# Dilated attention's query, key and value projections as seven block products, with the token sums on GpSimd

## The chip, the cores and the metric

One core of a Trainium2 chip runs the whole program. The metric is device microseconds of one execution; the kernel before was timed three times: 3373.47, 3375.91 and 3383.08 us, median 3375.91 us. All data are float32. In the trace a float32 matmul shows as two weight loads and two matmul passes (records of PEld and PE), so a count of passes is twice a count of matmuls.

## The reference, cut to what matters

The program computes two transformer blocks. The change lies in the second, where one 512 x 1024 activation `h` is multiplied by a wide weight matrix, and nine slices of 512 columns of the product are the dilated attention's queries (three slices), keys (three) and values (three); queries and keys are then turned by rotary angles.

```python
def rope(x, pos):
    hd = x.shape[-1]
    inv = ROPE_THETA ** (-jnp.arange(0, hd, 2, dtype=jnp.float32) / hd)
    ang = pos.astype(jnp.float32)[..., None] * inv
    ...
    return jnp.concatenate([x1 * cos - x2 * sin, x2 * cos + x1 * sin], axis=-1).astype(x.dtype)

def dilated_branch(dq, dk, dv, pos):
    B, S, _ = dq.shape
    shp = (B, S, DIL_GROUPS, DIL_HEADS, DIL_HD)
    q = rope(dq.reshape(shp), pos)
    k = rope(dk.reshape(shp), pos)
    v = dv.reshape(shp)
    ...

def second_block(x, positions, w_in, ...):
    for l in range(DEPTH_2):
        h = rmsnorm(x, pre_mix_g[l])
        z = h @ w_in[l]
        (g_q, g_k, g_v, g_o, a_low, sc_b, sc_c, sc_x,
         d_q, d_k, d_v) = jnp.split(z, split_points, axis=-1)
        y_gla = gla_branch(g_q, g_k, g_v, g_o, a_low, w_alpha_up[l], b_alpha[l], gla_norm_g[l])
        y_sc = sc_b * causal_dwconv(sc_c * sc_x, sc_conv_w[l])
        y_dil = dilated_branch(d_q, d_k, d_v, positions)
        ...
```

## The kernel before, in words

The program is a row of phases. Each phase is one block with a hand-written instruction list for each engine, and the engines meet between two phases. The last four phases are, with their stretches in the trace: `recurrent_phase` (L2007, to about 2326 us), `rope_phase` (L2406, 2326.8 to 2574), `merge_phase` (L2471, to 2882) and `feed_forward_phase` (L2692, from 2884 to the end).

`hT` holds the activation transposed: 128 partitions x 8 contraction blocks x 512 tokens. `ring` has two slots, each a weight job of 128 x 8 x 512 (2 MB). Jobs 0 to 5 are used in the recurrence, jobs 6 to 14 (`ROPE_JOB` = 6) in `rope_phase`, jobs from 15 (`GATE_JOB`) in the merge. SyncE issues job j once the last product of job j-2 is finished (L2424 to L2426).

`rope_phase` has 36 units, four to a job. The 24 query and key units have 128 weight columns as the stationary operand and 512 tokens as the moving one; the 12 value units have 128 tokens stationary and 512 weight columns moving. Each unit is eight matmuls over the contraction blocks into one of two PSUM banks `pa` (L2439, L2441). Of a query or key unit ScalarE copies the two halves of 64 partitions crosswise into `xs` (L2451, L2452), VectorE multiplies PSUM by `cos` (L2464) and `xs` by `sin` (L2465) and adds the two into `QK` (L2468). Of a value unit ScalarE copies PSUM to `dv` (L2456).

In `recurrent_phase` GpSimd clears two buffers and then, for each of four token tiles t, copies four diagonal blocks of `red` to `ST` (L2075) when VectorE has reduced them (L2283). TensorE runs the 128x512 products of jobs 2 to 5 (L2086) between the small products of the recurrence (L2121 to L2128, L2139 to L2146); its `weigh(t)` waits for the copies of tile t, for the state update (L2292, L2294) and for the norm (L2301, L2303) of tile t-1.

`merged` is a buffer of 128 x 8 x 512 that is first written in the merge phase.

The feed-forward phase of the kernel before already multiplies in the manner of the change: each of its 22 units is 28 matmuls of 128x256, seven products P1 to P7 of four contraction blocks each (L2824), from sums of weight blocks (VectorE L2983; for the first pair of units GpSimd L2751) and sums of token blocks. ScalarE copies P1 (L2906), and four VectorE additions of 512, 256, 512 and 512 elements (L2971 to L2974) make four output blocks of the seven products.

## Time and profile before

| what | value |
|---|---|
| three runs, median | 3375.91 us (3373.47 to 3383.08) |
| the profiled execution | 3380.27 us, its span 3378.5 us |
| TensorE matmul busy | 2861.0 us, 85% of the span |
| TensorE weight loads busy | 1655.1 us, 49% |
| VectorE busy | 1158.2 us, 34% |
| ScalarE busy | 767.0 us, 23% |
| GpSimd busy | 529.3 us, 16% |
| mean granted TensorE clock | 0.947 |

All numbers of the trace are of the one profiled execution. PE is TensorE's matmul record, PEld its weight load, DVE VectorE, ACT ScalarE, POOL GpSimd, SP SyncE; L2439 is line 2439 of the kernel. A time at which a row of the timeline starts is counted from the start of the span. Records that follow one another on an engine are merged into one row; the row's length is then that of the whole run of records, with the modelled end of the last. What stands in brackets is the idle time of the engine before the row and what released it.

### The profile page before, as it was taken

What the parts mean: (1) busy time and instruction counts of PE and PEld (TensorE: products, weight loads), DVE (VectorE), ACT (ScalarE), POOL (GpSimd) and SP (SyncE); (2) the same over time, 40 slices, a digit from 0 to 9 for tenths busy, and PEclk for the clock granted to TensorE, in tenths of its full rate; (3) what the DMA queues carried; (4) which work ended last, traced back from release to release, by engine and by line L of the source; (5) the groups of instructions that cost most, each with busy time, mean ns of one, the idle gap of its engine ahead of it and who ended that gap; (6) DMA issues with size and microseconds to landing.
All of it is one profiled execution on the core that took longest, in us unless ns stands there. A gap on an engine that the chain in (4) does not pass through costs nothing. (4 is left out here: it accounts for less than half of the span.)

```text
span 3378.5 us, 52188 instructions
## 1 busy us (share of the span) xinstructions
PE 2861.0 (85%) x21441; PEld 1655.1 (49%) x21441; DVE 1158.2 (34%) x2400; ACT 767.0 (23%) x1507; POOL 529.3 (16%) x660
## 2 busy tenths in 40 slices
PE   7998889588776798895867573999999999999999
PEld 4555655344343345653433332444444554588844
DVE  3424866312111343754111113533211231355501
ACT  2224651121111323630211112311112231111100
POOL 0003630233332001521322221000000000100000
PEclk8999999799999899996989886999999999999999
DMA  8733012999999552026999997112222112422337
GB/s 299 310 148 117 1 76 94 385 396 425 426 426 410 218 125 98 1 100 258 384 424 422 425 424 277 64 51 83 75 75 75 50 50 75 113 75 75 124 125 261
DMA packets 188531, 679.18 MB, mean 201 GB/s; under 512 B 52766, under 2 KB 94222, under 8 KB 163782
## 3 DMA queue, kind: packets, MB, share of 16 engines
q1 hardware_dynamic: 176446, 655.56, 49.9%
q0 software_dynamic: 11808, 21.03, 1.7%
q8 instruction: 131, 2.15, 0.3%
q14 instruction: 42, 0.34, 0.0%
q10 hardware_dynamic: 104, 0.10, 0.0%
HBM read 653.89 MB, written 33.98 MB: 204 GB/s over the span
## 5 line engine op out<-in xcount | busy, mean ns | idle before, releaser
L1719 PE MATMUL pH<-w,room 128*32 128x256 f32 x4224 | 253.3, 394 | 56.1 <-DMA w<-in_moe_w 55.6
L1756 DVE TENSOR_TENSOR hh<-hs,pH 128x128 f32<-128x128 f32 x118 | 34.0, 288 | 775.1 <-ACT hs L1739 775.1
L1719 PE MATMUL pH<-room 128*32 128x256 f32 x3328 | 211.7, 412 | 89.9 <-DMA room<-in_moe_w 66.9
L942 POOL TENSOR_SCALAR E<-E,st 128x768 f32<-128x768 f32 (+3 forms) x80 | 168.2, 2102 | 646.7 <-DVE st L1192 646.0
L1719 PEld LDWEIGHTS pH<-w,room 128*32 128x32 f32 x4224 | 140.9, 114 | 159.6 <-issue 79.3
L419 PE MATMUL pa<-aT,w 128*128 128x512 f32 x416 | 205.8, 599 | 1.3 <-DVE aT L693 1.3
L1719 PEld LDWEIGHTS pH<-room 128*32 128x32 f32 x3328 | 114.5, 119 | 179.7 <-issue 95.6
L1727 PE MATMUL pY<-w,hT 128*32 128x256 f32 x2112 | 130.4, 388 | 77.6 <-DVE hT L1759 60.9
L2534 PE MATMUL pa<-hT,ring 128*128 128x512 f32 x384 | 167.8, 592 | 0.0
L2439 PE MATMUL pa<-hT,ring 128*128 128x512 f32 x384 | 165.0, 592 | 1.3 <-PEq L91 1.3
L987 PE MATMUL pT<-ident,E 128*128 128x128 f32 x672 | 112.6, 286 | 55.0 <-ACT PT L1097 31.3
L2868 PE MATMUL banks<-ring,aT 128*128 128x512 f32 x352 | 151.2, 592 | 0.0
L1727 PE MATMUL pY<-room,hT 128*32 128x256 f32 x1664 | 100.6, 382 | 54.3 <-DVE hT L1759 54.3
L2086 PE MATMUL pa<-hT,ring 128*128 128x512 f32 x320 | 143.9, 606 | 0.0
L1017 PE MATMUL pS<-wout,oT 128*128 128x512 f32 x320 | 141.4, 594 | 0.8 <-issue 0.8
L1675 POOL DMA_INDIRECT y<-y,at_y x122 | 125.8, 1031 | 60.2 <-POOL at_y L1695 59.1
L1739 ACT ACTIVATE hs<-pH 128x128 f32<-128x128 f32 x118 | 32.7, 277 | 450.9 <-PE pH L1719 450.9
L1727 PEld LDWEIGHTS pY<-w,hT 128*32 128x32 f32 x2112 | 63.2, 111 | 144.0 <-DVE hT L1759 105.7
L1742 ACT ACTIVATE y<-pY 128x256 f32<-128x256 f32 x118 | 45.2, 383 | 346.5 <-PE pY L1727 343.7
L987 PEld LDWEIGHTS pT<-ident,E 128*128 128x128 f32 x672 | 71.2, 142 | 100.2 <-issue 47.6
L2439 PEld LDWEIGHTS pa<-hT,ring 128*128 128x128 f32 x384 | 72.9, 190 | 93.4 <-issue 93.4
L956 PE MATMUL pS<-room 64*128 64x256 f32 (+2 forms) x608 | 109.6, 477 | 8.3 <-ACT E L1086 4.9
(532 smaller groups left out, 4497.6 us busy)
## 6 DMA issues: line engine op xcount, KB each, us to landing
w<-in_moe_w SPq DMA_DIRECT2D x144, 2048.0 KB
room<-in_moe_w SPq DMA_DIRECT2D x48, 2048.0 KB
mw<-in_mod_w SPq DMA_DIRECT2D x24, 2048.0 KB, 16.6
ring<-in_w_ff_down SPq DMA_DIRECT2D x33, 1024.0 KB, 4.8
ring<-in_w_in SPq DMA_DIRECT2D x15, 2048.0 KB, 8.2
ring<-in_w_gate SPq DMA_DIRECT2D x6, 2048.0 KB, 8.4
wf<-in_w_ff_gate SPq DMA_DIRECT2D x11, 1024.0 KB, 5.7
wf<-in_w_ff_up SPq DMA_DIRECT2D x11, 1024.0 KB, 8.1
```

Of the source, the lines that this page charges most:

```text
L419: last = pe.matmul(pa[n % 2][:, 0:512], w[:, i % SLOTS_W, k, tile(c)], aT[:, k, 0:512], start=(k == 0), stop=(k == C - 1))
L942: pool.tensor_scalar(e, e, st[:, u % 4, 6 + b:7 + b], None, ALU.mult).then_inc(readyP, 1)
L956: return pe.matmul(pS[u % 2][:, at:at + w], qT[rows, p, tile(n)], kT[rows, k_chunk(p), k0:k0 + w], start=True, stop=True)
L987: last = pe.transpose(pT[:, tile(j)], E[:, u % NB, b, tile(i)], ident[:])
L1017: last = pe.matmul(pS[n % 2][:, half * 512:(half + 1) * 512], oT[:, k, tile(n)], wout[:, k, half * 512:(half + 1) * 512], start=(k == 4), ...
L1675: pool.indirect_dma_start(out=y_rows, out_offset=bass.IndirectOffsetOnAxis(ap=at_y[:, b:b + 1], axis=0), in_=y[:, b], in_offset=None, boun ...
L1719: last = pe.matmul(pH[strip(s), 0:2 * P].rearrange("p (j n) -> p j n", j=2), xT[:, k, :], slot_of(g, "w13", b)[:, :, k, s * P:(s + 1) * P] ...
L1727: last = pe.matmul(pY[strip(s), 0:YW], hT[:, k, :], slot_of(g, "w2", b)[:, k, s * YW:(s + 1) * YW], start=(k == 0), stop=(k == HC - 1))
L2086: last = pe.matmul(pa[b][:], ring[:, j % RING, i, tile(c)], hT[:, i, :], start=(i == 0), stop=(i == C - 1))
L2439: last = pe.matmul(pa[b][:], ring[:, j % RING, i, at], hT[:, i, :], start=(i == 0), stop=(i == C - 1))
L2534: last = pe.matmul(pa[b][:], ring[:, j % RING, k, (c % 4) * P:(c % 4 + 1) * P], hT[:, k, :], start=(k == 0), stop=(k == C - 1))
L2868: last = pe.matmul(banks[b][:, h * 512:(h + 1) * 512], aT[:, f, tile(t)], wd[:, m % SLOTS_D, f % 2, h * 512:(h + 1) * 512], start=(f == 0) ...
```

## The change

`rope_phase` is rewritten. A job's eight contraction blocks are split into `lo` and `hi`, its 512 weight columns into two halves, the 512 tokens into two halves. A job is now two units b = 0, 1 (128 columns of each column half; for the values 128 tokens of each token half). Each unit is seven products of four matmuls of 128x256, 28 matmuls in all, and gives the four 128x256 output blocks that two units gave before. The factors are blocks of `ring` and of `hT`, three sums of weight blocks in `S`, a fourth sum written over a weight block in place, and four sums of token blocks in `T`, which lies in `merged`.

VectorE makes the weight sums of a job (four additions of 128x1024; for the first job eight of 128x512) and turns each unit's seven products into outputs with four additions (`post`) in `Z`. Queries and keys are turned by three VectorE operations of 128x1024 for each unit, from `Z` instead of from PSUM, with two ScalarE copies of 64x1024 crosswise in between. Values go from `Z` to `dv` by two ScalarE copies. The four token sums are made by GpSimd in the recurrence, behind its copies of tile 1. `xs` and `Z` are single buffers, PSUM is double (two tensors of 1024 for each b). A ring slot is reloaded when `raised[1]`, the last product of its job, is counted.

```diff
--- before.py
+++ after.py
@@ -2004,7 +2004,7 @@
     return 16 * (j // RING + 1)
-def recurrent_phase(nc, g, hT, yT, cos, sin, rc):
+def recurrent_phase(nc, g, hT, yT, cos, sin, rc, T):
     BLK = 32
     SHORT = 6 * 2 * BLK
@@ -2035,8 +2035,8 @@
             ph.sem(n) for n in ("a_low", "a_moved", "raised", "logs", "rel", "exped", "inputs"))
         k_turned, k_moved, scored, d_taken, upper, reduced, diag_moved = (
             ph.sem(n) for n in ("k_turned", "k_moved", "scored", "d_taken", "upper", "reduced", "diag_moved"))
-        weighed, kv, stated, squared, meaned, rooted, normed, order_a = (
-            ph.sem(n) for n in ("weighed", "kv", "stated", "squared", "meaned", "rooted", "normed", "order_a"))
+        weighed, kv, stated, squared, meaned, rooted, normed, order_a, order_p = (
+            ph.sem(n) for n in ("weighed", "kv", "stated", "squared", "meaned", "rooted", "normed", "order_a", "order_p"))
         block = ph.block()
         ring, ring_in, ident = g["ring"], g["ring_in"], g["ident"]
@@ -2063,6 +2063,7 @@
         @block.gpsimd
         def _(pool):
+            step = Steps(pool, order_p)
             pool.memset(ST[:], 0.0).then_inc(zeroed, 1)
             pool.memset(S[:], 0.0).then_inc(zeroed, 1)
             pool.wait_ge(zeroed, 2)
@@ -2073,6 +2074,13 @@
                 for b in range(4):
                     rows = slice(b * BLK, (b + 1) * BLK)
                     pool.tensor_copy(ST[rows, t % 2, :, rows].rearrange("p (c b) i -> p b c i", b=2), red[rows].rearrange("p (b c i) -> p b c i", b=2, c=2)).then_inc(diag_moved, 1)
+                if t == 1:
+                    lo, hi, first, then = slice(0, C // 2), slice(C // 2, C), slice(0, LAT // 2), slice(LAT // 2, LAT)
+                    pool.wait_ge(diag_moved, 4 * t + 4)
+                    step(pool.tensor_tensor(T[:, 2], hT[:, hi, then], hT[:, lo, then], ALU.subtract))
+                    step(pool.tensor_tensor(T[:, 0], hT[:, lo, then], hT[:, lo, first], ALU.subtract))
+                    step(pool.tensor_tensor(T[:, 1], hT[:, hi, then], T[:, 0], ALU.subtract))
+                    step(pool.tensor_tensor(T[:, 3], hT[:, hi, first], T[:, 1], ALU.subtract))
         @block.tensor
         def _(pe):
@@ -2403,16 +2411,43 @@
             conv_out(3)
-def rope_phase(nc, g, hT, QK, dv, cos, sin, mask, gate_bias):
+def block_sums(eng, w, s, n0, n1):
+    half = w.shape[2] // 2
+    lo, hi = slice(0, C // 2), slice(C // 2, C)
+    a, b, to = slice(n0, n1), slice(half + n0, half + n1), slice(n0, n1)
+    return ((s[:, 0, :, to], w[:, lo, b], w[:, hi, b], ALU.add), (s[:, 1, :, to], s[:, 0, :, to], w[:, lo, a], ALU.subtract),
+            (s[:, 2, :, to], w[:, hi, a], s[:, 1, :, to], ALU.subtract), (w[:, lo, b], w[:, lo, a], w[:, lo, b], ALU.subtract))
+def rope_phase(nc, g, hT, QK, dv, cos, sin, mask, gate_bias, T):
+    HT, HN = LAT // 2, 256
+    lo, hi = slice(0, C // 2), slice(C // 2, C)
+    NQK, NV = 6, 3
     with Phase(nc) as ph:
-        xs, t1, t2 = ph.sb("xs", [P, 2, LAT]), ph.sb("t1", [P, 2, LAT]), ph.sb("t2", [P, 2, LAT])
-        pa = [ph.ps(f"pa{b}", [P, 512]) for b in range(2)]
-        product, taken, x_ready, x_used = (ph.sems(k) for k in ("product", "taken", "x_ready", "x_used"))
-        order, mask_in = ph.sem("order"), ph.sem("mask_in")
+        S = ph.sb("S", [P, 2, 3, C // 2, HN])
+        Z = ph.sb("Z", [P, 8, HT])
+        xs = ph.sb("xs", [P, 2, LAT])
+        banks = [ph.ps(f"banks{i}", [P, 1024]) for i in range(4)]
+        raised, taken, posted = (ph.sems(k) for k in ("raised", "taken", "posted"))
+        x_ready, x_used, s_made, order, mask_in = (ph.sem(n) for n in ("x_ready", "x_used", "s_made", "order", "mask_in"))
         block = ph.block()
         ring, ring_in = g["ring"], g["ring_in"]
-        NQK, NV = 24, 12
+        flat = Z[:].rearrange("p z n -> p (z n)")
+        outputs = flat[:, HT:5 * HT].rearrange("p (a n) -> p a n", a=2)
+        def weights(q):
+            return ring[:, (ROPE_JOB + q) % RING]
+        def place_of(b, name):
+            i, at = {"P6": (0, 0), "P2": (0, HT), "P1": (0, 512), "P7": (0, 512 + HT), "P3": (1, 0), "P4": (1, HT), "P5": (1, 512)}[name]
+            return banks[2 * b + i][:, at:at + HT]
         @block.sync
         def _(sp):
@@ -2422,50 +2457,99 @@
                 sp.dma_start(mask[s][:], g["dil_mask"][s][t * P:(t + 1) * P, 0:w * P]).then_inc(mask_in, 16)
             sp.dma_start(gate_bias[:], g["b_gate_2"][0].rearrange("(k p) -> p k", p=P), allow_slow_non_contiguous=True).then_inc(mask_in, 16)
             for j in range(ROPE_JOB + 2, GATE_JOB + 2):
-                sp.wait_ge(product[1], 2 * (j - 2 - ROPE_JOB) + 2)
+                sp.wait_ge(raised[1], j - 1 - ROPE_JOB)
                 load_weights(sp, g, j)
             sp.wait_ge(mask_in, 64)
         @block.tensor
         def _(pe):
-            for n in range(NQK + NV):
-                b, j, c = n % 2, ROPE_JOB + n // 4, n % 4
-                if n >= 2:
-                    pe.wait_ge(taken[b], n // 2)
+            def products(q, b, names):
+                w, s, unit = weights(q), S[:, q % 2], slice(b * P, (b + 1) * P)
+                first, then = slice(0, HT), slice(HT, LAT)
+                factors = {"P1": (w[:, lo, 0:HN], hT[:, lo, first]), "P2": (w[:, hi, 0:HN], hT[:, hi, first]), "P3": (s[:, 2], hT[:, hi, then]),
+                           "P4": (w[:, hi, HN:], T[:, 3]), "P5": (s[:, 0], T[:, 0]), "P6": (s[:, 1], T[:, 1]), "P7": (w[:, lo, HN:], T[:, 2])}
+                for name in names:
+                    of_w, of_x = factors[name]
+                    for k in range(C // 2):
+                        at_w, at_x = (of_w[:, k, unit], of_x[:, k]) if q < NQK else (of_x[:, k, unit], of_w[:, k])
+                        last = pe.matmul(place_of(b, name), at_w, at_x, start=(k == 0), stop=(k == C // 2 - 1))
+                return last
+            for q in range(NQK + NV):
+                j = ROPE_JOB + q
                 pe.wait_ge(ring_in[j % RING], loads_of(j))
-                at = slice(c * P, (c + 1) * P)
-                for i in range(C):
-                    if n < NQK:
-                        last = pe.matmul(pa[b][:], ring[:, j % RING, i, at], hT[:, i, :], start=(i == 0), stop=(i == C - 1))
-                    else:
-                        last = pe.matmul(pa[b][:], hT[:, i, at], ring[:, j % RING, i, :], start=(i == 0), stop=(i == C - 1))
-                last.then_inc(product[b], 1)
+                for b in range(2):
+                    if q:
+                        pe.wait_ge(posted[b], q)
+                    products(q, b, ("P1", "P2"))
+                    pe.wait_ge(s_made, q + 2 if q else b + 1)
+                    products(q, b, ("P6", "P7", "P5", "P4", "P3")).then_inc(raised[b], 1)
         @block.scalar
         def _(act):
-            for n in range(NQK):
-                b = n % 2
-                act.wait_ge(product[b], n // 2 + 1)
-                if n >= 2:
-                    act.wait_ge(x_used[b], n // 2)
-                act.activation(xs[0:64, b], pa[b][64:P, :], ACT.Copy)
-                act.activation(xs[64:P, b], pa[b][0:64, :], ACT.Copy).then_inc(x_ready[b], 1)
-            for n in range(NQK, NQK + NV):
-                b, m = n % 2, n - NQK
-                act.wait_ge(product[b], n // 2 + 1)
-                act.activation(dv[:, m % 4, m // 4, :], pa[b][:], ACT.Copy).then_inc(taken[b], 1)
+            for q in range(NQK + NV):
+                for b in range(2):
+                    act.wait_ge(raised[b], q + 1)
+                    if q:
+                        act.wait_ge(posted[b], q)
+                    act.activation(Z[:, 6 + b], place_of(b, "P1"), ACT.Copy).then_inc(taken[b], 1)
+                    act.wait_ge(posted[b], q + 1)
+                    if q < NQK:
+                        if q or b:
+                            act.wait_ge(x_used, 2 * q + b)
+                        act.activation(xs[0:64], outputs[64:P], ACT.Copy)
+                        act.activation(xs[64:P], outputs[0:64], ACT.Copy).then_inc(x_ready, 1)
+                    else:
+                        for i in range(2):
+                            last = act.activation(dv[:, b::2, q - NQK, i * HN:(i + 1) * HN], outputs[:, i].rearrange("p (a n) -> p a n", a=2), ACT.Copy)
+                        last.then_inc(x_ready, 1)
         @block.vector
         def _(dve):
             step = Steps(dve, order)
-            for n in range(NQK):
-                b = n % 2
-                dve.wait_ge(x_ready[b], n // 2 + 1)
-                dve.tensor_tensor(t1[:, b], pa[b][:], cos[:], ALU.mult).then_inc(taken[b], 1)
-                dve.tensor_tensor(t2[:, b], xs[:, b], sin[:], ALU.mult).then_inc(x_used[b], 1)
-                dve.wait_ge(taken[b], n // 2 + 1)
-                dve.wait_ge(x_used[b], n // 2 + 1)
-                dve.tensor_tensor(QK[:, n], t1[:, b], t2[:, b], ALU.add)
+            def twice(x, n):
+                return x.rearrange("p (o n) -> p o n", o=1).broadcast_to([P, 2, n])
+            def sums(q, which, n0=0, n1=HN):
+                if q >= NQK + NV:
+                    return
+                j = ROPE_JOB + q
+                dve.wait_ge(ring_in[j % RING], loads_of(j))
+                for k in which:
+                    out, in0, in1, op = block_sums(dve, weights(q), S[:, q % 2], n0, n1)[k]
+                    last = dve.tensor_tensor(out, in0, in1, op)
+                    if k == 3:
+                        last.then_inc(s_made, 1)
+                    else:
+                        step(last)
+            def post(q, b):
+                dve.wait_ge(taken[b], q + 1)
+                if q or b:
+                    dve.wait_ge(x_ready, 2 * q + b)
+                step(dve.tensor_tensor(Z[:, 0:2], twice(Z[:, 6 + b], HT), banks[2 * b][:, 0:512].rearrange("p (a n) -> p a n", a=2), ALU.add))
+                step(dve.tensor_tensor(Z[:, 5], Z[:, 0], place_of(b, "P7"), ALU.add))
+                step(dve.tensor_tensor(Z[:, 0:5:4], Z[:, 0:6:5], twice(place_of(b, "P5"), HT), ALU.add))
+                dve.tensor_tensor(Z[:, 2:4], Z[:, 0:6:5], banks[2 * b + 1][:, 0:512].rearrange("p (a n) -> p a n", a=2), ALU.add).then_inc(posted[b], 1)
+            for b in range(2):
+                sums(0, range(4), b * P, (b + 1) * P)
+            for q in range(NQK + NV):
+                for b in range(2):
+                    post(q, b)
+                    if b == 0:
+                        sums(q + 1, range(1 if q else 0, 4))
+                    if q < NQK:
+                        to = QK[:, 4 * q + b:4 * q + b + 3:2]
+                        dve.wait_ge(posted[b], q + 1)
+                        dve.tensor_tensor(to, outputs, twice(cos[:], LAT), ALU.mult)
+                        dve.wait_ge(x_ready, 2 * q + b + 1)
+                        step(dve.tensor_tensor(xs[:], xs[:], twice(sin[:], LAT), ALU.mult))
+                        dve.tensor_tensor(to, to, xs[:], ALU.add).then_inc(x_used, 1)
+                    if b:
+                        sums(q + 2, (0,))
 def merge_phase(nc, g, hT, yT, QK, dv, merged, mask, bias):
@@ -3068,6 +3152,7 @@
                 return stack.enter_context(nc.sbuf_tensor(name, shape, F32))
             hT, merged = keep2("hT", [P, C, LAT]), keep2("merged", [P, C, LAT])
+            T = merged[:].rearrange("p k n -> p (k n)").rearrange("p (i k n) -> p i k n", i=4, k=C // 2)
             g["ring"] = keep2("ring", [P, RING, C, 512])
             with ExitStack() as branches:
                 yT = keep2("yT", [P, 12, LAT], branches)
@@ -3078,11 +3163,11 @@
                         ("count", [P, 32], F32), ("token", [P, NTILE], F32), ("pos", [P, LAT], I32), ("inv", [P, 1], F32),
                         ("cw", [P, 3, 4], F32), ("gv", [P, NLAT, 512], F32))}
                     combine_turn_phase(nc, g, DEPTH - 1, share, g["pre_mix_g_2"], hT, rc)
-                    recurrent_phase(nc, g, hT, yT, cos, sin, rc)
+                    recurrent_phase(nc, g, hT, yT, cos, sin, rc, T)
                 QK, dv = keep2("QK", [P, 24, LAT], branches), keep2("dv", [P, NLAT, 3, 512], branches)
                 mask = [keep2(f"dil_mask{s}", [P, w * P], branches) for s, w in ((0, 2), (1, 4), (2, 4))]
                 gate_bias = keep2("gate_bias", [P, 24], branches)
-                rope_phase(nc, g, hT, QK, dv, cos, sin, mask, gate_bias)
+                rope_phase(nc, g, hT, QK, dv, cos, sin, mask, gate_bias, T)
                 merge_phase(nc, g, hT, yT, QK, dv, merged, mask, gate_bias)
             feed_forward_phase(nc, g, merged, hT)
```

## Rows read from the trace of the kernel before

**Rows 1.** The page: span and busy time of TensorE.

```profile
span 3378.5 us, 52188 instructions
PE 2861.0 (85%) x21441; PEld 1655.1 (49%) x21441; DVE 1158.2 (34%) x2400; ACT 767.0 (23%) x1507; POOL 529.3 (16%) x660
```

**Rows 2.** Windows: length, busy PE, PEld, DVE, ACT, POOL, then clock, DMA share, GB/s.

```profile
2326.80:2573.90 247.10, 247.10 (x576) 109.32 (x576) 47.58 (x72) 34.91 (x59) 0.00 (x0) 1.00 0.24 79
...
3010.00:3260.00 250.00, 250.00 (x1068) 202.62 (x1067) 121.88 (x159) 32.88 (x54) 0.00 (x0) 1.00 0.30 98
```

**Rows 3.** Timeline of both ends of `rope_phase`: start, length, engine, line, operands, idle before.

```profile
2326.79 17.41 PE L2439 MATMUL pa<-hT,ring 128*128 128x512 f32 x40 [1.27 <-PEq L91]
...
2333.93 0.59 ACT L2451 ACTIVATE xs<-pa 64x512 f32<-64x512 f32 x1 [14.55 <-PE pa L2439]
...
2574.26 0.60 ACT L2456 ACTIVATE dv<-pa 128x512 f32<-128x512 f32 x1 [6.27 <-PE pa L2441]
...
2575.49 0.91 PE L2552 MATMUL pS<-QK 128*128 128x128 f32 x6 [1.26 <-PEq L91]
```

**Rows 4.** Timeline, one unit of the feed-forward phase's up products.

```profile
3099.82 0.69 DVE L2971 TENSOR_TENSOR r<-r,banks 128x512 f32<-128x512 f32 x1 [3.80 <-ACT r L2906]
...
3111.42 0.38 ACT L2906 ACTIVATE r<-banks 128x256 f32<-128x256 f32 x1 [5.93 <-PE banks L2824]
3111.91 0.69 DVE L2971 TENSOR_TENSOR r<-r,banks 128x512 f32<-128x512 f32 x1 [1.91 <-ACT r L2906]
...
3113.80 0.69 DVE L2974 TENSOR_TENSOR r<-r,banks 128x512 f32<-128x512 f32 x1
...
3114.53 0.81 ACT L2908 ACTIVATE xg<-r,cw 128x512 f32<-128x512 f32 x1 [2.72 <-DVE r L2974]
```

**Rows 5.** The instructions that touch S: ns min/median/max, first and last start.

```profile
L2983 DVE TENSOR_TENSOR S<-S,wf x10: 1218/1218/1225, 2970.0 to 3186.9; 128x1024 f32<-128x1024 f32 x10
```

**Rows 6.** ScalarE's crosswise copy; landing of the transfers into ring, 2320 to 2540 us.

```profile
L2451 ACT ACTIVATE xs<-pa x24: 593/593/593, 2333.9 to 2491.9; 64x512 f32<-64x512 f32 x24
...
DMA to landing us min/median/max: 7.9/8.2/9.7
```

**Rows 7.** Timeline of the recurrence about the place of the token sums.

```profile
2239.49 1.32 POOL L2075 COPY ST<-red 32x128 f32<-32x128 f32 x4 [33.58 <-DVE red L2283]
...
2243.56 1.43 DVE L2294 SCALAR_TENSOR_TENSOR S<-S,dn,pK 64x128 f32<-64x128 f32 x4 [4.13 <-PE pK L2146]
...
2252.26 3.35 DVE L2301 RECIPROCAL rt<-rt 128x512 f32<-128x512 f32 x1 [7.27 <-ACT rt L2224]
...
2262.52 1.32 POOL L2075 COPY ST<-red 32x128 f32<-32x128 f32 x4 [21.71 <-DVE red L2283]
...
2275.40 0.39 PE L2139 MATMUL pO<-ST,rc_gv 128*128 128x128 f32 x2
```

**Rows 8.** Timeline: GpSimd's 128x1024 additions beside a VectorE addition, feed-forward phase.

```profile
2904.23 2.35 POOL L2751 TENSOR_TENSOR S<-wf 128x1024 f32<-128x1024 f32 x1 [604.01 <-DMA wf<-in_w_ff_up]
2904.43 3.23 DVE L2955 TENSOR_TENSOR x<-x,r 128x1024 f32<-128x1024 f32 x1
...
2906.66 3.22 POOL L2751 TENSOR_TENSOR S<-S,wf 128x1024 f32<-128x1024 f32 x1
```

**Rows 9.** Timeline of TensorE: same-sized runs of passes with and without idle before.

```profile
2226.46 14.00 PE L2086 MATMUL pa<-hT,ring 128*128 128x512 f32 x32
...
2257.77 0.53 PE L2125 MATMUL pD<-A 64*32 64x32 f32 x11 [4.54 <-issue]
...
2258.85 16.71 PE L2086 MATMUL pa<-hT,ring 128*128 128x512 f32 x32
...
2884.27 29.40 PE L2800 MATMUL banks<-ring,merged 128*128 128x512 f32 x64 [2.07 <-PEq L91]
...
2975.28 6.60 PE L2824 MATMUL banks<-hT,wf 128*128 128x256 f32 x16 [3.45 <-DVE wf L2983]
```

**Rows 10.** Windows behind the idle time of 4.54 us; columns as in rows 2.

```profile
2257.70:2262.00 4.30, 4.23 (x23) 2.40 (x23) 2.03 (x3) 0.91 (x3) 0.00 (x0) 0.50 0.10 35
```

**Rows 11.** Waits, 2960 to 3220 us: who for whom, total us, times, longest.

```profile
DVE S L2983 <- DMA wf<-in_w_ff_up: 26.5, 8, 4.1
```

## The prediction

> **What bounds the kernel now.** I read the page first: TensorE is busy for 85% of a span of 3378.5 us and no other engine for more than 34% [rows 1]. Busy shares are means over stages, so the windows come next. In the whole of `rope_phase` TensorE is busy for 247.1 of 247.1 us at full granted clock, while VectorE has 47.6 and ScalarE 34.9 us of work and the DMA engines are used to 0.24 [rows 2]. So this stage is bound by the number of TensorE passes and by nothing else, and what it is worth to remove a pass is its full time. The timeline at both ends gives the beat: from ScalarE's first copy at 2333.93 to its last at 2574.26 lie 35 units, 6.867 us each, 16 passes of 512 columns; TensorE idles 1.27 us before the phase and 1.26 us behind it [rows 3]. The profiled execution took 3380.27 us for that span, 4.4 us above the median of 3375.91. I sum against the profiled one and move the result by that.
>
> **The products.** 36 units at 6.867 us are 247.2 us. The new form of a unit exists in this kernel already: the feed-forward phase runs 28 matmuls of 128x256 to a unit, with the same PSUM layout, the same copy of P1 and the same four additions, and two neighbouring units there start their first addition at 3099.82 and 3111.91, 12.09 us apart [rows 4], with TensorE busy for 250 of 250 us at full clock over twenty units [rows 2]. 18 units at 12.09 are 217.6 us. The gain is 29.6 us, just under the eighth (30.9) that seven for eight products promise. The near rows leave little doubt here; only the value units, with tokens stationary, are new in this form, and before the change both orientations kept one beat (the 35 intervals include both) [rows 3].
>
> The Trainium skill, TensorE: Matmul & The Clock Gate, section Back-to-back issue gap, charges each matmul pass a fixed 2.5 ns beside its columns, which speaks against shorter passes: 1008 instead of 576 would cost an estimated 1.1 us of the eighth. The beat of 12.09 us for 56 passes, 215.9 ns each against 429.2 for the double width, agrees and has it in already.
>
> **VectorE, hidden.** One weight sum of 128x1024 takes 1.22 us [rows 5]; four for a job are 4.9, with gaps 5.0. One `post` takes 2.58 us, from 3111.91 to the end of L2974 [rows 4]; two are 5.2. The rotary operations are now three of 128x1024 for each unit; nearest is again the 1.22 us addition, so 7.4 us. That is 17.6 us of the 24.2 us of a query or key job and 10.2 of a value job: cover remains, 6.6 us at least. The order leaves room too, counting from the last product of job q. TensorE needs `posted` of a bank pair one whole unit (12.1 us) later, and `post` is done after 3.1 us, so 9 us are spare. Behind unit 1 VectorE turns (to about 7.7 us, with a wait for ScalarE's copies, at most 2 x 1.19 us by doubling the 0.593 row [rows 6]) and then waits for the load of job q+2, issued at time 0. Loads into the ring land after 7.9 to 9.7 us [rows 6]; the first sum ends by 11 us, the next `post` is due at 12.5. VectorE stands in that same wait in the feed-forward phase, 8 times with at most 4.1 us [rows 11], with its beat unharmed [rows 4]. The other three sums end near 19 us and are needed at 12.1 + 12.1 + 3.45 of this count, 27.6. So the landing could be some 8 us later before TensorE felt it. ScalarE has 2.8 us for each unit. Cost: nothing.
>
> **The start.** TensorE's first eight matmuls (P1, P2, 16 passes, 3.45 us) need no sums. VectorE makes four half-width sums meanwhile, at 0.69 us and 0.03 between them (the 512-wide addition) [rows 4], 2.9 us. Value 0, up to 0.5 if VectorE leaves the meeting of the engines late. Job 6 was loaded long before.
>
> **The end.** Before, the phase ended with one ScalarE copy of 0.60 us [rows 3]. Now the last unit has ScalarE's copy of P1, four additions and two copies. From the start of the copy of P1 to ScalarE's next start behind the additions are 3.11 us (3111.42 to 3114.53) [rows 4], and two copies of 512 elements, 0.60 each as before, follow: 4.3 us instead of 0.6, so +3.7 (3.5 to 4.7). Nothing hides this, for the next phase starts behind a meeting of all engines: TensorE is idle for 1.26 + 3.7 = 5.0 us.
>
> **The clock behind that idle.** This is the term that one overlooks. Behind 4.54 us of idle the window has a granted clock of 0.50 [rows 10], the lower level of 1.2 GHz, and 32 passes take 16.71 instead of 14.00 us, +2.7. Behind 3.45 us, 16 passes take 6.60 instead of 3.45 (12.09 x 16/56) with an overhang of 0.2, +3.0. Behind 2.07 us, 64 passes take 29.40, where twice 14.00 less an overlap of 0.2 is 27.8, +1.6 [rows 9]. Behind 1.26 us there is no loss [rows 2, 3]. With 5.0 us of idle I take +2.8, between 1.6 and 3.1.
>
> The Trainium skill, the same page, section HAM oscillation, warns of TensorE idle times in just this way; a sum without it would end 2.8 us lower, which is the second rival.
>
> **GpSimd's token sums, hidden.** They start behind the copies of tile 1, at 2239.49 + 1.32 = 2240.8. Four additions of 128x1024 take 2.35 us each alone, up to 3.22 with company [rows 8]: 9.7 to 13.2 us, so they end at 2250.5 to 2254. GpSimd's next duty is tile 2 at 2262.5 [rows 7], 8 us later; nobody else waits for its queue. What they can stretch is VectorE: an addition with company took 3.23 us instead of 1.22 [rows 5, 8]. In that stretch VectorE runs only `state(1)`, four small operations at 2243.56. If each stood behind a whole GpSimd addition, it would end at 2253 instead of 2245 and push the reciprocal at 2252.26 by a microsecond; both feed `weigh(2)` at 2275.4 [rows 7], 20 us later. Cost 0 from both sides: the products of that stretch leave TensorE no idle for a gain either.
>
> The Trainium skill, SBUF — State Buffer, section Who interferes with whom, would have VectorE and GpSimd block each other only where the VectorE operation has two SBUF inputs; `state(1)` has one and a PSUM input, so by it even that stretching does not come. The 3.23 us [rows 8] is an addition with two, and agrees.
>
> **The sum.** -29.6 + 3.7 + 2.8 = -23.1 us. No DMA is added; the ring loads have the same size and order. 3380.3 - 23.1 = 3357.2 by the profiled execution, 3352.8 by the median.
>
> **Rivals.**
> 1. *The clock stays up at the end.* For it: 1.26 us of idle cost nothing. Against: 5.0 us is longer than all three idle times [rows 9], and each of those cost. Gives 3350.0. Chance 0.10.
> 2. *TensorE runs dry while a ring load is in flight.* In the recurrence TensorE stood still for 4.54 us with nothing to wait for ("issue") [rows 9]; the change issues 1.75 times the passes, beside nine loads. One such stop with its clock loss is 4.54 + 2.7 = 7.2 us. One for each load gives -23.1 + 65 = +42, 3418, slower; it decides from four stops on, two or three end within the measurement. Against: that stop came amid hundreds of 64x32 products, and the feed-forward phase has the new rate and 2 MB loads with no stop in 250 us [rows 2]. Chance 0.07, half of it slower.
> 3. *VectorE becomes the bound.* Its ten 128x1024 operations of a query or key job would have to take 3.23 us [rows 8], by their layout (a broadcast operand, outputs 2 units apart, in place): 32 + 5.2 = 37.5 us against 24.2, +80 us over six jobs, 3433. It turns the forecast to a loss once a job takes 28 us, that is 2.3 us an operation. Against: `post` has broadcast and strided operands at the normal price, and GpSimd has no work here. Chance 0.03.
> 4. *The products pay less,* by waits of a few tenths for each unit that the feed-forward phase doesn't have (single `xs` and `Z`, a wait for both banks): 18 x 0.8 = 14 us would bring the change to -9, 3367, no measurable difference. Chance 0.05.
>
> The forecast itself has 0.75.
>
> **How the numbers follow.** Forecast 3353. Its own terms reach from -25.5 to -20.5; the three runs of before spread by 2.4 below and 7.2 above their median. With rival 1 inside, that is 3346 to 3362; outside it lie rivals 2 to 4, 0.15. About 0.3%, 10 us, is what a measurement of this kernel can tell from no change. Faster: 0.75 + 0.10 and the few single stops of rival 2, 0.87; same 0.07; slower 0.06.
>
> **What would show it.** Right: `rope_phase` has 1008 passes in about 217.9 us, TensorE never idle in it, `post` starts 12.1 us apart in query, key and value jobs alike; 5.0 us of idle before the merge's first scores, and half the clock behind it, with the first 32 gate passes at 16.5 us; GpSimd's four additions between 2241 and 2254 us and `weigh(2)` not moved. Wrong: idle of TensorE on `s_made` or `posted` inside the phase, VectorE operations of 128x1024 above 1.3 us, sums that end after the next unit's second product, or a late `weigh(2)`.

## The result and the profile after

The changed kernel takes 3356.15 us (median of four runs, 3353.08 to 3358.63) against 3379.49 us of the kernel before (four runs, 3373.47 to 3383.76): ratio 0.9928, 95% interval 0.9916 to 0.9940, that is 23.3 us less. In a second session it was 3355.6 against 3379.99 us, 0.9932 (0.9919 to 0.9946). The profiled execution took 3354.14 us.

The page of the changed kernel, its span and busy times:

```profile
span 3352.3 us, 53098 instructions
...
PE 2833.0 (85%) x21873; PEld 1738.4 (52%) x21873; DVE 1239.9 (37%) x2476; ACT 770.7 (23%) x1501; POOL 538.7 (16%) x664
```

Beside [rows 1], TensorE has 28.0 us less to do with 432 passes more, and VectorE 81.7 us more. TensorE's share stays at 85%: the share doesn't show what was won.

Windows of the changed kernel (length; busy PE, PEld, DVE, ACT, POOL; clock, DMA share, GB/s): the new `rope_phase`, the stretch behind it, and two stretches of the merge phase.

```profile
2324.57:2542.30 217.73, 217.73 (x1008) 191.41 (x1008) 129.11 (x144) 37.61 (x51) 0.00 (x0) 1.00 0.27 90
2542.30:2546.90 4.60, 0.07 (x2) 0.03 (x1) 2.48 (x4) 1.57 (x4) 0.00 (x0) 0.83 0.65 215
2546.90:2550.00 3.10, 3.10 (x8) 2.09 (x9) 1.58 (x5) 1.58 (x2) 0.00 (x0) 0.50 0.92 355
2550.00:2554.00 4.00, 4.00 (x8) 1.77 (x7) 0.58 (x2) 1.65 (x3) 0.00 (x0) 0.73 0.01 3
```

The phase takes 217.7 instead of 247.1 us [rows 2], TensorE is never idle in it, and VectorE's work went from 47.6 to 129.1 us. Behind it TensorE stands for 4.5 us without work, and then runs at half the clock (0.50, the level of 1.2 GHz).

The timeline of both ends of the phase, which answers to [rows 3]:

```profile
2324.57 3.69 PE L2475 MATMUL banks<-hT,ring 128*128 128x256 f32 x16 [1.27 <-PEq L91]
2328.10 1.89 PE L2475 MATMUL banks<-merged,S 128*128 128x256 f32 x8
...
2542.41 0.38 ACT L2495 ACTIVATE Z<-banks 128x256 f32<-128x256 f32 x1 [7.90 <-PE banks L2475]
2542.82 0.69 DVE L2532 TENSOR_TENSOR Z<-Z,banks 128x512 f32<-128x512 f32 x1 [9.50 <-ACT Z L2495]
...
2544.72 0.69 DVE L2535 TENSOR_TENSOR Z<-Z,banks 128x512 f32<-128x512 f32 x1
2545.44 1.15 ACT L2504 ACTIVATE dv<-Z 128x512 f32<-128x512 f32 x2 [2.65 <-DVE Z L2535]
...
2546.90 1.62 PE L2636 MATMUL pS<-QK 128*128 128x128 f32 x6 [4.53 <-PEq L91]
...
2548.31 15.80 PE L2618 MATMUL pa<-hT,ring 128*128 128x512 f32 x32
...
2563.95 1.46 PE L2636 MATMUL pS<-QK 128*128 128x256 f32 x6
```

P6 follows P1 and P2 with no gap, so the first sums were in time. At the other end one sees the chain that ScalarE and VectorE now run alone: copy, four additions, two copies. Its counterpart before is the single copy of [rows 3], and in the merge phase these two rows:

```profile
2576.23 13.90 PE L2534 MATMUL pa<-hT,ring 128*128 128x512 f32 x32
...
2589.97 1.46 PE L2552 MATMUL pS<-QK 128*128 128x256 f32 x6
```

Three marks divide the difference. From the phase's first pass to ScalarE's first copy of the last unit: 247.47 us before, 217.84 after, -29.63. From there to the merge's first score: 1.23 and 4.49, +3.26. From there to the second group of scores: 14.48 and 17.05, +2.57. Together that is -23.80 us. The spans differ by 26.2: 2.2 more lie ahead of the phase (its start at 2326.79 and 2324.57) and 0.2 behind. The 2.2 are scatter as far as the profiles show: in those whose recurrence is that of either kernel the phase starts anywhere from 2324.0 to 2329.8 us (2326.7 to 2329.8 with the old phase, 2324.0 to 2329.3 with the new one), and the last 86 us ahead of it are equal (85.92 before, 86.07 after).

VectorE in the second unit of the first job and at the next `post`, timeline:

```profile
2352.06 1.22 DVE L2547 TENSOR_TENSOR QK<-Z,cos 128x1024 f32<-128x1024 f32 x1
2354.21 1.23 DVE L2549 TENSOR_TENSOR xs<-xs,sin 128x1024 f32<-128x1024 f32 x1 [0.93 <-ACT xs L2501]
2355.47 1.22 DVE L2550 TENSOR_TENSOR QK<-QK,xs 128x1024 f32<-128x1024 f32 x1
2357.08 1.23 DVE L2521 TENSOR_TENSOR S<-ring 128x1024 f32<-128x1024 f32 x1 [0.39 <-DMA ring<-in_w_in]
2361.58 0.69 DVE L2532 TENSOR_TENSOR Z<-Z,banks 128x512 f32<-128x512 f32 x1 [3.27 <-ACT Z L2495]
```

The operations with a broadcast or in-place operand cost the 1.22 us of [rows 5]. The wait for the load is 0.39 us, and VectorE stands free for 3.27 us before the next `post`.

### The profile page after: what moved, and what is told of

The parts are those of the page before. It is cut to its first block and busy times, and to the rows that moved or that the text cites. A ratio compares the mean times of both kernels' runs of the same rounds, so it can differ in the third digit from the quotient of the medians.

```text
span 3352.3 us, 53098 instructions
## 1 busy us (share of the span) xinstructions
PE 2833.0 (85%) x21873; PEld 1738.4 (52%) x21873; DVE 1239.9 (37%) x2476; ACT 770.7 (23%) x1501; POOL 538.7 (16%) x664
## 5 line engine op out<-in xcount | busy, mean ns | idle before, releaser
L2618 PE MATMUL pa<-hT,ring 128*128 128x512 f32 x384 | 169.7, 598 | 0.0
L2094 PE MATMUL pa<-hT,ring 128*128 128x512 f32 x320 | 143.8, 606 | 0.0
L2952 PEld LDWEIGHTS banks<-ring,aT 128*128 128x128 f32 x352 | 66.9, 190 | 83.8 <-issue 83.7
```

The source lines that it names most:

```text
L2094: last = pe.matmul(pa[b][:], ring[:, j % RING, i, tile(c)], hT[:, i, :], start=(i == 0), stop=(i == C - 1))
L2618: last = pe.matmul(pa[b][:], ring[:, j % RING, k, (c % 4) * P:(c % 4 + 1) * P], hT[:, k, :], start=(k == 0), stop=(k == C - 1))
L2952: last = pe.matmul(banks[b][:, h * 512:(h + 1) * 512], aT[:, f, tile(t)], wd[:, m % SLOTS_D, f % 2, h * 512:(h + 1) * 512], start=(f == 0) ...
```

## Experiments

All but the last change one thing, and all but two start from the changed kernel. Since the stretches ahead of `rope_phase` scatter by more than most effects, each is also read between two marks of its own trace: from the first pass of `rope_phase` to the merge's first score (222.33 us in the changed kernel), to its second group of scores (239.38 us), or from the first pass of `weigh(1)` (tile 1 of the recurrence, L2147, at 2238.50 us) to the first pass of `rope_phase` (86.07 us).

**The changed kernel again**, beside the next three.

> The changed kernel once more, as the yardstick for the runs beside it. Theory: 23 to 26 us below the kernel before, ratio 0.992 to 0.9935; rope_phase 217.7 us, 4.5 us of TensorE idle behind it, the first 32 gate passes of the merge in 15.8 us.

Measured 3355.6 us (five runs, 3354.24 to 3359.3), ratio 0.9932 (0.9919 to 0.9946). Its trace repeats the marks: 222.33 us to the first score and 239.36 to the second group.

**Idle matmuls behind the last product.**

```diff
                     products(q, b, ("P6", "P7", "P5", "P4", "P3")).then_inc(raised[b], 1)
+            pe.wait_ge(posted[0], NQK + NV)
+            for i in range(4):
+                pe.matmul(banks[0][:, 0:512], hT[:, i, 0:P], hT[:, i, :], start=True, stop=True)
```

> The changed kernel with four matmuls of 128x512 more on TensorE behind the last product of rope_phase, into a PSUM bank that nobody reads any more. They take 8 x 0.429 = 3.4 us and end 1.1 us before the merge can start. Theory (the clock falls because TensorE is idle for 4.5 us): from the last product to the first score as before (4.5 us), but the scores take 0.9 instead of 1.6 us and the first 32 gate passes 13.9 to 14.0 instead of 15.8, 2.6 us less than the changed kernel. Rival (the first passes are slow for another reason, the 2 MB load that starts at the same time or a cold start of the phase): the passes stay at 15.8 us and the time is that of the changed kernel.

Measured 3352.0 us (3349.82 to 3354.45), 3.6 less than the changed kernel beside it. Timeline of TensorE at the end:

```profile
2541.86 3.60 PE L2489 MATMUL banks<-hT 128*128 128x512 f32 x8
...
2546.55 0.91 PE L2639 MATMUL pS<-QK 128*128 128x128 f32 x6 [1.09 <-PEq L91]
...
2547.29 13.90 PE L2621 MATMUL pa<-hT,ring 128*128 128x512 f32 x32
...
2561.03 1.46 PE L2639 MATMUL pS<-QK 128*128 128x256 f32 x6
```

The window behind the start of the scores, columns as above:

```profile
2546.50:2550.00 3.50, 3.45 (x13) 2.05 (x14) 2.03 (x7) 2.67 (x4) 0.00 (x0) 1.00 0.84 323
```

The first score comes 222.32 us behind the first pass, as in the changed kernel, and the second group after 236.80, 2.58 us less. The 2 MB load is in flight as before (DMA share 0.84), and still the clock is 1.00 and the passes take 13.90. So TensorE's own idle time is the cause of the slow passes, and this run measures the clock term of the prediction alone. The rest of the 3.6 us is not accounted for. In this trace the feed-forward phase starts at full clock behind its 2.07 us of idle (64 passes in 27.71 us), and in the changed kernel's it doesn't (29.40); but that difference also appears between kernels that are equal there (last section), and it can't be put down to the edit.

**The last unit by plain products.**

```diff
+                    if (q, b) == (LAST, 1):
+                        for i, t in enumerate((1, 3)):
+                            for k in range(C):
+                                last = pe.matmul(banks[2][:, i * 512:(i + 1) * 512], hT[:, k, t * P:(t + 1) * P], weights(q)[:, k], start=(k == 0), stop=(k == C - 1))
+                            last.then_inc((plain, raised[1])[i], 1)
+                        continue
...
+                    if (q, b) == (LAST, 1):
+                        act.wait_ge(plain, 1)
+                        act.activation(dv[:, 1, q - NQK, :], banks[2][:, 0:512], ACT.Copy)
+                        act.wait_ge(raised[1], q + 1)
+                        act.activation(dv[:, 3, q - NQK, :], banks[2][:, 512:1024], ACT.Copy)
+                        continue
```

> The changed kernel, but its very last unit (values, b = 1) is made by plain products, two sums of eight matmuls of 128x512, and copied from PSUM straight to dv by ScalarE; the fourth weight sum of that job goes to the free xs buffer, so that the weights stay whole. Theory: the unit costs 32 x 0.429 = 13.7 us instead of 12.1, +1.6; the end of the phase is again one ScalarE copy, TensorE idle 1.3 instead of 4.5 us, -3.2; no clock loss behind it, -2.6. Together 4.2 us less than the changed kernel. Rival (the end hides behind something else, such as the 2 MB load for the merge): only +1.6 shows.

Measured 3351.13 us (3347.1 to 3354.08), 4.5 less than the changed kernel beside it. Timeline:

```profile
2546.83 0.60 ACT L2504 ACTIVATE dv<-banks 128x512 f32<-128x512 f32 x1 [6.27 <-PE banks L2489]
...
2548.05 0.91 PE L2654 MATMUL pS<-QK 128*128 128x128 f32 x6 [1.26 <-PEq L91]
...
2548.79 13.90 PE L2636 MATMUL pa<-hT,ring 128*128 128x512 f32 x32
...
2562.53 1.46 PE L2654 MATMUL pS<-QK 128*128 128x256 f32 x6
```

To the second group of scores it is 235.19 us (2327.34 to 2562.53), 4.19 less, where 4.2 were expected. The seven-product form loses in this phase's last unit: it saves 1.6 us of passes there and costs 5.8, of which 3.2 are idle time and 2.6 are clock.

**The token sums on VectorE at the start of the phase.**

```diff
-                    step(pool.tensor_tensor(T[:, 2], hT[:, hi, then], hT[:, lo, then], ALU.subtract))
...
+            step(dve.tensor_tensor(T[:, 2], hT[:, hi, then], hT[:, lo, then], ALU.subtract))
+            step(dve.tensor_tensor(T[:, 0], hT[:, lo, then], hT[:, lo, first], ALU.subtract))
+            step(dve.tensor_tensor(T[:, 1], hT[:, hi, then], T[:, 0], ALU.subtract))
+            step(dve.tensor_tensor(T[:, 3], hT[:, hi, first], T[:, 1], ALU.subtract))
             for b in range(2):
                 sums(0, range(4), b * P, (b + 1) * P)
```

> The changed kernel with the four token sums made by VectorE at the start of rope_phase instead of by GpSimd in the recurrence. VectorE needs 4 x 1.25 + 4 x 0.72 = 7.9 us before TensorE may go on behind P1 and P2 (3.5 us). Theory: 4.4 us of TensorE idle on s_made, and 2.7 us of clock loss behind it, +7.1 us over the changed kernel. Rival 1: the idle alone, +4.4. Rival 2 (GpSimd's additions cost something in the recurrence that goes away here): the recurrence gets shorter and the sum lies below +4.4.

Measured 3362.14 us (four runs, 3360.42 to 3363.74), 6.5 more than the changed kernel. Timeline:

```profile
2331.98 3.78 PE L2468 MATMUL banks<-merged,S 128*128 128x256 f32 x8 [4.28 <-DVE ring L2514]
2335.55 2.39 PE L2468 MATMUL banks<-merged,ring 128*128 128x256 f32 x8
2337.78 1.89 PE L2468 MATMUL banks<-merged,S 128*128 128x256 f32 x8
```

TensorE is idle for 4.28 us on the fourth weight sum, and it takes 229.11 instead of 222.33 us to the first score, +6.78. The 16 passes behind the stop take 5.80 us from start to start (2331.98 to 2337.78) instead of 3.46, so 2.3 us are clock. From `weigh(1)` to the phase it is 85.95 us instead of 86.07, so rival 2 of this expectation falls. That is what the move to GpSimd is worth: it hides 5 us of VectorE that would cost 7.

**The token sums alone**, added to the kernel before.

> The kernel before with GpSimd's four token sums in the recurrence and nothing else of the change (the sums are not used). Theory: they end 10 us before GpSimd's next duty and stretch nothing, so 0 us against the kernel before, within 1 us in the trace of the recurrence. Rival (they hold up VectorE's state update or GpSimd's next copies): weigh(2) comes late and the recurrence is 1 to 3 us longer.

Measured 3380.14 us (eleven runs) against 3379.93, ratio 1.000 (0.999 to 1.0009). GpSimd and VectorE in the recurrence, timeline:

```profile
2240.60 2.36 POOL L2080 TENSOR_TENSOR merged<-hT 128x1024 f32<-128x1024 f32 x1
...
2243.26 1.43 DVE L2302 SCALAR_TENSOR_TENSOR S<-S,dn,pK 64x128 f32<-64x128 f32 x4 [4.13 <-PE pK L2154]
...
2247.89 2.34 POOL L2083 TENSOR_TENSOR merged<-hT,merged 128x1024 f32<-128x1024 f32 x1
...
2262.55 1.32 POOL L2076 COPY ST<-red 32x128 f32<-32x128 f32 x4 [12.31 <-issue]
```

The state update lies fully beside GpSimd's additions and takes the same 1.43 us as in [rows 7]; the additions take 2.35 us each, none is stretched.

**More work for VectorE**: in each query and key unit the multiplication by `cos` is made n/2 times more, n = 4 and n = 8 to a job.

```diff
+                        for i in range(n // 2):
+                            step(dve.tensor_tensor(to, outputs, twice(cos[:], LAT), ALU.mult))
                         dve.tensor_tensor(to, outputs, twice(cos[:], LAT), ALU.mult)
```

> The changed kernel with four more VectorE operations of 128x1024 in each query or key job (each unit's multiplication by cos is made three times instead of once). Theory (VectorE has 6.6 us of cover in a job of 24.2): 4 x 1.26 = 5.0 us are hidden, the time is that of the changed kernel within 1 us, TensorE never idle in the phase. Rival (the order of the waits, not the sum of work, limits: posted or s_made comes late): idle of TensorE in each of six jobs, 5 us and more in all.

> The same with eight more (five times instead of once in each unit), 10.1 us. Theory (VectorE becomes the bound once a job needs over 24.2 us): 17.6 + 10.1 = 27.7 us and up to 1 us of waits for ScalarE and transfers, so 3.5 to 4.5 us over in each job, 21 to 27 us in six, less some 9 us of head start that posted has, 12 to 20 us more than the changed kernel; the gain of the change is then mostly gone. Rival (VectorE works beside TensorE with more cover than counted): under 5 us. Rival (each late post also costs clock): over 30 us.

With four: 3357.18 us (four runs), and 222.33 us to the first score, as without. TensorE has no idle time in the phase: 30 us more of VectorE (5.0 in each of six jobs) are free. With eight: 3367.75 us (3363.3 to 3368.32), 234.14 us to the first score, +11.8. TensorE's idle times are six:

```profile
2412.37 3.72 PE L2475 MATMUL banks<-hT,ring 128*128 128x256 f32 x16 [0.89 <-DVE Z L2535]
...
2439.54 5.41 PE L2475 MATMUL banks<-hT,ring 128*128 128x256 f32 x16 [2.16 <-DVE Z L2535]
...
2493.87 5.41 PE L2475 MATMUL banks<-ring,hT 128*128 128x256 f32 x16 [2.16 <-DVE Z L2535]
```

They add up to 6.6 us; two of them, of 2.16 us, are followed by 5.41 instead of 3.69 us for 16 passes, 3.4 us of clock; the last 1.8 are about 0.17 us at each stop, which lie under the modelled end of the row before it, and one or two tenths in the passes behind it. The first stop comes at 2412, 86 us into the phase: the head start lasts three and a half jobs. `post` of unit 0 in two following jobs, timeline of VectorE:

```profile
2422.18 0.69 DVE L2532 TENSOR_TENSOR Z<-Z,banks 128x512 f32<-128x512 f32 x1
...
2449.34 0.69 DVE L2532 TENSOR_TENSOR Z<-Z,banks 128x512 f32<-128x512 f32 x1
```

VectorE waits for nothing there and needs 27.17 us for a job, 3.0 over TensorE's 24.17, where 3.5 to 4.5 were expected; that is why the size is just under the 12 to 20. The reserve of 9 us was right: the `post` that TensorE waits for at its first stop begins at 2409.73, 9.9 us behind its place in a beat of 12.09, and the stop is 0.9 us.

**The ring loads one unit later.**

```diff
                 sp.wait_ge(raised[1], j - 1 - ROPE_JOB)
+                if j < GATE_JOB:
+                    sp.wait_ge(raised[0], j - ROPE_JOB)
                 load_weights(sp, g, j)
```

> The changed kernel with each ring load of the phase issued one unit (12.1 us) later, so that it lands 20.3 instead of 8.2 us behind the end of its job's predecessor. Theory (the landing had some 8 us to spare, VectorE then waits for it and hands on posted and s_made just late): counted through the waits, a job needs 8.2 + 1.25 + 2.6 + 3.8 + 8.6 = 24.5 us instead of 24.2, so 0.3 us in each of seven jobs, 2 to 4 us in all, short idle of TensorE on s_made. Rival (the landing had no room): 4 us or more in each job, 28 us and more. Rival (still hidden): nothing.

Measured 3360.73 us (3358.61 to 3362.37); 225.90 us to the first score, +3.57. VectorE's first wait for a load grows by one unit, from 0.39 to 12.56 us:

```profile
2373.95 1.23 DVE L2523 TENSOR_TENSOR S<-ring 128x1024 f32<-128x1024 f32 x1 [12.56 <-DMA ring<-in_w_in]
```

The loss is 0.5 us in each of seven jobs, in short waits of TensorE on `posted` and on the fourth sum. So 12.1 us of delay are half a microsecond more than a job can take, and in the changed kernel the landing has some 11.6 us to spare (an estimate: 12.1 less 3.57 / 7).

**Narrow passes in the kernel before**: each matmul of 128x512 as two of 128x256.

> The kernel before with each matmul of 128x512 in rope_phase made as two of 128x256 into the halves of the bank, so 1152 passes instead of 576 for the same sums, nothing else changed. Theory (a pass has a small cost beside its columns, 215.9 ns for 256 against 429.2 for 512): a unit takes 6.91 instead of 6.87 us, the phase 1.4 us longer, 249 instead of 247.5 us from its first product to ScalarE's last copy. Rival (the weight loads of 0.19 us limit passes of 256): clearly over 2 us.

One run, so only its trace is read. The units follow at 6.907 us (ScalarE's first copy of the first unit at 2337.02, of the last at 2578.76) instead of 6.867, and from first pass to last copy it is 248.92 instead of 247.47, +1.45 us. 576 passes more cost 2.5 ns each. The passes of the seven products are as dear (215.9 ns, and 6.907 us / 32 = 215.8 here).

**The load of job 5 behind levels(2).** TensorE stands still for 4.5 to 5.2 us in the recurrence in each kernel so far, within the small products of tile 2, `levels(2)`. This run takes the load away from there.

```diff
                 sp.wait_ge(product[1], use(n) // 2 + 1)
+                if j == 5:
+                    sp.wait_ge(scored, 3)
                 load_weights(sp, g, j)
```

> The changed kernel, with the ring load of job 5 in the recurrence issued only when the small products of levels(2) are finished, some 2 us later. In all kernels so far TensorE stands still for 4.5 to 5.2 us within levels(2), with nothing to wait for, while that 2 MB load is in flight and one packet of instructions falls into the same stretch. Theory (TensorE's next instructions queue behind the load, rival 2 of the prediction at the place where it is real): the stop shrinks to under 1 us and the clock loss of 2.7 us behind it goes, 6 to 7.5 us less than the changed kernel. Rival (the stop comes from the many small products alone): it stays at 4.5 us or more and nothing changes.

Measured 3348.89 us (four runs, 3345.79 to 3352.45), ratio 0.9906 (0.989 to 0.9923); 80.68 us instead of 86.07 from `weigh(1)` to the phase, -5.4. Timeline of the stop, and the window behind it:

```profile
2258.98 0.38 PE L2135 MATMUL pD<-A 64*32 64x32 f32 x11 [2.42 <-issue]
...
2258.90:2262.00 3.10, 3.02 (x25) 1.72 (x25) 2.70 (x6) 0.91 (x3) 0.00 (x0) 1.00 0.23 26
```

Neither theory holds whole. The stop stays, but halved, 2.42 instead of 4.82 us, and the clock behind it stays up. (Behind the stop, the load is issued at 2259.83, some 6 us later than otherwise, not 2.) The lines of the DMA queues (packets, MB, share) in the changed kernel from 2249 to 2257 us, and then in this one from 2254 to 2260 us:

```profile
q1 hardware_dynamic: 1037, 2.09, 78.1%
q8 instruction: 2, 0.03, 1.8%
```

```profile
q8 instruction: 1, 0.02, 1.4%
```

Here one packet of instructions moves with nothing beside it. So about 2.4 us of the stop come without a load, and about as much again goes away with it. That the packet is what TensorE waits for is an inference from the place; no run shows it.

**Three edits together**: the plain last unit, the later load, and one idle matmul at the end of the merge phase.

```diff
+            pe.wait_ge(taken[0], 24)
+            pe.matmul(pa[0][:], hT[:, 0, 0:P], hT[:, 0, :], start=True, stop=True)
```

> Three edits on the changed kernel: the last unit of rope_phase by plain products, the load of job 5 behind levels(2), and one idle 128x512 matmul at the end of the merge phase, so that TensorE stands still for 1.3 instead of 2.07 us before the feed-forward phase. Theory: -4.2 us, -7 us, and -1.6 us if the clock loss behind 2.07 us is avoided; together some 12 us less than the changed kernel, about 3344 us, ratio to the kernel before 0.989 to 0.990. Rival (the gains overlap or are given back): under 8 us.

Measured 3343.48 us (four runs, 3338.6 to 3349.39), ratio 0.9891 (0.9872 to 0.991), some 12 us below the 3355.6 of the changed kernel, which wasn't timed beside it. This version beats both kernels. The first two edits account for 9.6 us between the marks of their own traces (4.19 and 5.39); what the third gives isn't shown, since three kernels without it also start the feed-forward phase at full clock.

## Why the prediction was right

**The products** (-29.6). Measured -29.63. The beat of 12.09 us, taken from the feed-forward phase, held for query, key and value jobs alike; the narrow passes show the part of the eighth that is lost to the number of passes. It is 30.9 - 29.6 = 1.3 us, 504 passes more than seven eighths of 576, where the prediction's estimate of 1.1 counted 432.

**VectorE hidden.** Right that it is hidden. Its sum of 17.6 of 24.2 us was 0.5 too high: eight operations more (10.1 us) make a job of 27.17, so it needs 17.1 without them. The two runs with more work enclose the limit: 5 us more in a job are free, 10 are not. ScalarE's crosswise copies take 1.06 us each, inside the bound of 1.19. The margin for the landing was larger than the 8 us counted, some 11.6: the count, 27.6 - 19 = 8.6, took the latest landing, 9.7 instead of 8.2 us, and left out the 1.5 us that VectorE stands free behind the first sum.

**The start** (0 to 0.5). 0: the fourth sum of the first half ends at 2327.4, P6 begins at 2328.1. With 5 us more ahead of them (the token sums on VectorE) the price appears at once.

**The end** (+3.7). Measured +3.26, below its bounds of 3.5 to 4.7, and TensorE is idle for 4.53 instead of 5.0 us. The chain itself was right (4.18 us from the copy of P1 to the end of the last copy, where 4.3 were counted); the step from ScalarE's end to the next phase is 0.31 instead of 0.63 us. In the changed kernel SyncE issued its last load well before that end, in the kernel before at the same moment as ScalarE's copy. The run with the plain last unit has the load beside the last copy again, and the step is 0.62 us again; that fits, but nothing else was tried on it.

**The clock** (+2.8, bounds 1.6 to 3.1). Measured +2.57 and, alone, 2.58 by the idle matmuls. The first 32 gate passes take 15.80 us and not the 16.5 given as a sign, because part of the slow stretch is spent in the scores ahead of them (1.62 instead of 0.91). The bounds were needed: behind the same 4.53 us of idle the run with the later load lost only 1.7 us, 16.16 us from the first to the second scores against 14.48:

```profile
2547.21 1.16 PE L2638 MATMUL pS<-QK 128*128 128x128 f32 x6 [4.53 <-PEq L91]
...
2563.37 1.46 PE L2638 MATMUL pS<-QK 128*128 128x256 f32 x6
```

Rival 1, without the term, would have been 2.6 us off here and is shown wrong by the run with idle matmuls. (The prediction once calls it the second rival; the first of its list is meant.)

**GpSimd's sums** (0). Right, ratio 1.000 for the sums alone. Four VectorE operations with one SBUF and one PSUM input were not stretched beside GpSimd's additions, 1.43 us with and without. That bears out the harmless side of the Trainium skill's rule on the shared port (SBUF — State Buffer, section Who interferes with whom); the rule makes an exception of VectorE's two-port modes, and no run here tests those. The prediction's wider bound, a whole GpSimd addition before each, wasn't needed.

**Rival 2**, TensorE running dry, is real in one place of the recurrence and not in `rope_phase`, where 1008 passes beside nine loads show no stop. What the prediction had wrong was its nature: it priced 4.54 us as the effect of a load in flight, and half of it comes without one.

**The sum.** -23.8 between the marks against -23.1: the end and the clock were put 0.4 and 0.2 us too high. 3356.15 us against a forecast of 3353, which stood on the three runs then known, 3.6 us below the median of the four of this comparison. Against those four the change is -23.3 us; that it meets -23.1 within 0.2 is luck, for the interval of the ratio allows 20 to 28 us. The forecast's reach of its own terms, -25.5 to -20.5, doesn't follow from their bounds, which give -24.5 to -21.3; -23.8 lies in both.

## What to carry to other kernels

Where a stage is bound by one engine at full clock, and another stage of the same kernel runs the new form already, take the gain from its beat per unit (here 29.6 us, measured 29.63); what remains to be worked out is the two ends of the stage. Look there for the chain that the other engines run alone behind the last product, and charge the idle time twice, once itself and once as clock. The cheap remedies are to make the last unit in the form with the shortest tail, or to give TensorE idle matmuls that end just before the next stage can start.

## What the runs showed of the hardware that was not expected

The clock's loss behind an idle time of a given length is not one number. Behind 4.53 us it was 2.57 us in one kernel and 1.7 in another. Behind 2.07 us, at the start of the feed-forward phase, the same 64 passes took 29.40 us in nine of twelve traces, both of the changed kernel among them, and 27.7 in three: with idle matmuls behind `rope_phase`, with the plain last unit, and with narrow passes. All are the same there. Timeline of the changed kernel, then of the narrow passes:

```profile
2858.26 29.40 PE L2884 MATMUL banks<-ring,merged 128*128 128x512 f32 x64 [2.07 <-PEq L91]
```

```profile
2888.76 27.70 PE L2801 MATMUL banks<-ring,merged 128*128 128x512 f32 x64 [2.07 <-PEq L91]
```

What decides between the two isn't shown. Behind 2.42 us in the recurrence the window shows a clock of 1.00. Behind 1.26 us no run showed a loss. So the idle times of 2.1 to 2.4 us cost between nothing and 1.7 us, and those of 3.45 to 4.54, with [rows 9], between 1.7 and 3.0.

TensorE stood still within the small products of levels(2), with nothing to wait for, in each profile: 4.5 to 5.2 us in the eleven where a 2 MB load was in flight, 2.42 and 2.36 us in the two where it wasn't. The same group of products for another tile, with the load of job 6 issued just before it, has no such stop. What makes it fall where it does stays open.
